# Up-projection of the latents in a two-block transformer kernel: each token tile scaled right behind its own sums of squares, tile 0 transposed while the last tile is scaled

## The reference, cut to what matters

```python
def rms_norm(x, g):
    y = xf * lax.rsqrt(jnp.mean(xf * xf, axis=-1, keepdims=True) + EPS)
    return (y * g.astype(jnp.float32)).astype(x.dtype)
def latent_attention(cq, ckv, k_rope, pos, g_cq, w_q_up, g_ckv, w_kv_up, g_qn, g_qr, g_kn, g_kr):
    ...
    q = (rms_norm(cq, g_cq) @ w_q_up).reshape(B, S, H, MLA_NOPE + MLA_ROPE)
    q_nope = rms_norm(q[..., :MLA_NOPE], g_qn)
    q_rot = rope(rms_norm(q[..., MLA_NOPE:], g_qr), pos)
    kv = (rms_norm(ckv, g_ckv) @ w_kv_up).reshape(B, S, H, MLA_NOPE + MLA_V)
    k_nope = rms_norm(kv[..., :MLA_NOPE], g_kn)
    v = kv[..., MLA_NOPE:]
    k_rot = rope(rms_norm(k_rope, g_kr), pos)
    ...
```

## Time and profile before

| | us |
|---|---|
| median of 3 runs | 3315.81 |
| lowest and highest of them | 3313.59, 3319.44 |
| the profiled execution, its own time | 3311.89 |
| its span in the trace | 3310.1 |
| `latent_up_phase`, layer 0, stretch 2097.9 to 2140.8 | 42.9 |
| `latent_up_phase`, layer 1, stretch 2791.0 to 2831.5 | 40.5 |

### The profile page before, as it was taken

The page is one execution under the profiler, slowest core; times in us unless marked ns, Lnnn a source line. Parts: engine busy times, 40 slices in busy tenths (PEclk is TensorE's granted clock), DMA queues, the critical chain, the costliest instruction groups (busy, mean ns, idle before and its releaser), DMA issues. The chain is left out here.

```text
span 3310.1 us, 50960 instructions
## 1 busy us (share of the span) xinstructions
PE 3045.4 (92%) x21910; PEld 2363.7 (71%) x21910; DVE 1610.3 (49%) x2276; ACT 1294.7 (39%) x1991; POOL 118.4 (4%) x215
## 2 busy tenths in 40 slices
PE   7996787799999898999999988899999898989999
PEld 5753666677777776677777776577888775678887
DVE  5313665455354448745454448654333467553332
ACT  3213343243233433743233344555333336544241
POOL 0200000010000000010000010100000100000000
PEclk9997778799999999999999989999999999999999
DMA  4310000154553222254543221012332320032322
GB/s 140 102 51 17 4 4 4 66 162 131 176 155 122 73 89 83 72 157 139 178 140 134 81 89 53 1 46 84 101 98 93 97 80 1 1 99 93 102 91 88
DMA packets 224241, 289.10 MB, mean 87 GB/s; under 512 B 7968, under 2 KB 163912, under 8 KB 217873
## 3 DMA queue, kind: packets, MB, share of 16 engines
q1 hardware_dynamic: 213728, 226.26, 21.8%
q0 software_dynamic: 8704, 55.39, 4.9%
q10 hardware_dynamic: 1584, 4.19, 0.3%
HBM read 281.62 MB, written 2.10 MB: 86 GB/s over the span
## 5 line engine op out<-in xcount | busy, mean ns | idle before, releaser
L226 DVE TENSOR_TENSOR weights_low_all<-weights,weights_high_all 128x2048 fp32r<-128x2048 f32 x196 | 450.0, 2296 | 584.8 <-ACT weights_high_all L220 577.2
L220 ACT CAST weights_high_all<-weights 128x2048 fp32r<-128x2048 f32 x196 | 373.6, 1906 | 575.2 <-PE ps L234 573.1
L232 PE MATMUL ps<-ffn_h_high,weights_high_all 128*128 128x512 f32 x704 | 278.4, 395 | 0.9 <-DVE weights_low_all L226 0.9
L233 PE MATMUL ps<-ffn_h_low,weights_high_all 128*128 128x512 f32 x704 | 274.9, 390 | 0.0
L234 PE MATMUL ps<-ffn_h_high,weights_low_all 128*128 128x512 f32 x704 | 274.8, 390 | 0.0
L232 PE MATMUL ps<-mlp_h_high,weights_high_all 128*128 128x512 f32 x512 | 200.8, 392 | 3.5 <-DVE weights_low_all L226 1.8
L234 PE MATMUL ps<-mlp_h_high,weights_low_all 128*128 128x512 f32 x512 | 199.4, 389 | 0.0
L233 PE MATMUL ps<-mlp_h_low,weights_high_all 128*128 128x512 f32 x512 | 199.3, 389 | 0.0
L232 PE MATMUL ps<-weights_high_all,mlp_hid_high 128*128 128x512 f32 x512 | 199.2, 389 | 0.0
L233 PE MATMUL ps<-weights_low_all,mlp_hid_high 128*128 128x512 f32 x512 | 199.2, 389 | 0.0
L234 PE MATMUL ps<-weights_high_all,mlp_hid_low 128*128 128x512 f32 x512 | 199.2, 389 | 0.0
(11 more groups left out here) (549 smaller groups left out, 6232.6 us busy)
## 6 DMA issues: line engine op xcount, KB each, us to landing
mod_w<-in_w_mod POOLq DMA_DIRECT2D x48, 1024.0 KB, 5.1
weights<-in_ffn_w_up SPq DMA_DIRECT2D x88, 512.0 KB, 5.0
weights<-in_w_mlp_in SPq DMA_DIRECT2D x32, 1024.0 KB, 5.5
weights<-in_w_mlp_out SPq DMA_DIRECT2D x32, 1024.0 KB, 4.9
weights<-in_ffn_w_down SPq DMA_DIRECT2D x24, 768.0 KB, 4.5
weights<-in_mix_w_in SPq DMA_DIRECT2D x13, 1024.0 KB, 5.2
weights<-in_na_w_qkv SPq DMA_DIRECT2D x12, 1024.0 KB, 5.1
weights<-in_w_in SPq DMA_DIRECT2D x12, 1024.0 KB, 5.4
```

The source lines that it names most:

```text
L220: nc.scalar.copy(st.high[s][:], st.raw[s][:]).then_inc(st.high_done, 1)
L226: nc.vector.tensor_tensor(st.low[s][:], st.raw[s][:], st.high[s][:], ALU.subtract).then_inc(st.split_done, 1)
L232: nc.tensor.matmul(out, lh, rh, start=start, stop=False)
L233: nc.tensor.matmul(out, lh, rl, start=False, stop=False)
```

## The change

Six things change, all inside `latent_up_phase`:

1. DVE calls `apply(t)` right behind the sums of tile t, no longer one tile later.
2. ACT takes the three square roots of a tile before the copy of its values; DVE waits for that copy (`v_done`) ahead of the key scaling.
3. ACT loads the square-root table at the phase's start, by a square root of one column into a spare tile.
4. POOL starts on a tile after its first scaling (`3 * t + 1`) and not after its third.
5. The transposes of tiles 0, 1 and 2 share banks 0 to 3, and those of tile 3 get banks 4 to 7 (`turn_bank`). So tile 0 waits for tile 2 to leave its banks, tiles 1 and 2 wait for the copy-out of the tile before, and tile 3 for its own scaling.
6. The copy-out of tile 0 moves forward: on DVE between the sums and the `apply` of tile 3, on ACT one group ahead of the roots of tile 3 and one behind.

```diff
+    def turn_bank(t, n):
+        return n + (4 if t == TT - 1 else 0)
@@ tensor
             for t in range(TT):
                 pe.wait_ge(rotated, 2 * t + 2)
+                if t in (0, TT - 1):
+                    up = 2 if t == 0 else TT - 1
+                    pe.wait_ge(scaled, 3 * (up + 1))
+                    pe.wait_ge(v_done, up + 1)
                 for n in range(4):
-                    b = (4 * t + n) % 8
-                    if t < 2:
-                        if n == 0:
-                            pe.wait_ge(scaled, 3 * (t + 3))
-                            pe.wait_ge(v_done, t + 3)
-                    else:
-                        pe.wait_ge((out_act, out_dve)[n % 2], 2 * (t - 2) + n // 2 + 1)
+                    if t in (1, 2):
+                        pe.wait_ge((out_act, out_dve)[n % 2], 2 * (t - 1) + n // 2 + 1)
@@ scalar
+            nc.scalar.activation(cx.spare[:], cx.ones[:, 0:1], ACT.Sqrt)
...
+                if t == TT - 1:
+                    put_out(0, 0)
+                roots(t)
                 nc.scalar.copy(v[:, t, :].rearrange("p (b h c) -> p b h c", b=2, h=4), heads(b + 2, P, 64, 64)).then_inc(v_done, 1)
-                roots(t)
+            put_out(0, 2)
@@ vector, in apply
+                dve.wait_ge(v_done, t + 1)
                 nc.vector.tensor_tensor(by_bank(k_tok[:, t, :, 0:64]), heads(b + 2, P, 0, 64), factor(t, 1, 64), ALU.mult)\
@@ vector, the loop
-                if t:
-                    apply(t - 1)
-            apply(TT - 1)
-            for t in range(TT):
+                if t == TT - 1:
+                    put_out(0)
+                apply(t)
+            for t in range(1, TT):
@@ gpsimd
-                pool.wait_ge(scaled, 3 * t + 3)
+                pool.wait_ge(scaled, 3 * t + 1)
```

More of the change, by code:

```diff
@@ L2927, in _ @@
                 pe.wait_ge(rotated, 2 * t + 2)
+                if t in (0, TT - 1):
+                    up = 2 if t == 0 else TT - 1
+                    pe.wait_ge(scaled, 3 * (up + 1))
+                    pe.wait_ge(v_done, up + 1)
                 for n in range(4):
-                    b = (4 * t + n) % 8
-                    if t < 2:
-                        if n == 0:
-                            pe.wait_ge(scaled, 3 * (t + 3))
-                            pe.wait_ge(v_done, t + 3)
-                    else:
-                        pe.wait_ge((out_act, out_dve)[n % 2], 2 * (t - 2) + n // 2 + 1)
+                    if t in (1, 2):
+                        pe.wait_ge((out_act, out_dve)[n % 2], 2 * (t - 1) + n // 2 + 1)
                     for h in range(4):
                         src = (q_tok, k_tok)[n // 2][:, t, 4 * (n % 2) + h, :]
-                        mm = nc.tensor.transpose(ps[0:96, b, h * P:(h + 1) * P], src, cx.ident[:])
+                        mm = nc.tensor.transpose(ps[0:96, turn_bank(t, n), h * P:(h + 1) * P], src, cx.ident[:])
                     mm.then_inc(turned, 1)
@@ L2942, in put @@
             dst = (qT, kT)[n // 2][0:96, 4 * (n % 2):4 * (n % 2) + 4, t * P:(t + 1) * P]
-            return dst, ps[0:96, (4 * t + n) % 8, :].rearrange("p (h c) -> p h c", h=4), column(cx, f"mla_{'qk'[n // 2]}{l}", 0)[0:96]
+            return dst, ps[0:96, turn_bank(t, n), :].rearrange("p (h c) -> p h c", h=4), column(cx, f"mla_{'qk'[n // 2]}{l}", 0)[0:96]
         @block.scalar
         def _(act):
+            nc.scalar.activation(cx.spare[:], cx.ones[:, 0:1], ACT.Sqrt)
             for n in (0, 2):
@@ L2956, in roots, with put_out @@
                         .then_inc(rooted, 1)
+            def put_out(t, n):
+                act.wait_ge(turned, 4 * t + n + 1)
+                dst, src, gain = put(t, n)
+                nc.scalar.activation(dst, src, ACT.Identity, scale=gain).then_inc(out_act, 1)
             for t in range(TT):
@@ L2965, in _ @@
                 nc.scalar.activation(by_bank(sq_k[t % 2]), heads(b + 2, P, 0, 64), ACT.Square).then_inc(k_sq, 1)
+                if t == TT - 1:
+                    put_out(0, 0)
+                roots(t)
                 nc.scalar.copy(v[:, t, :].rearrange("p (b h c) -> p b h c", b=2, h=4), heads(b + 2, P, 64, 64)).then_inc(v_done, 1)
-                roots(t)
-            for t in range(TT):
+            put_out(0, 2)
+            for t in range(1, TT):
                 for n in (0, 2):
-                    act.wait_ge(turned, 4 * t + n + 1)
-                    dst, src, gain = put(t, n)
-                    nc.scalar.activation(dst, src, ACT.Identity, scale=gain).then_inc(out_act, 1)
+                    put_out(t, n)
         @block.vector
@@ L2977, in _, with put_out @@
             nc.vector.tensor_scalar(cT[:, 1, :], ps[:, 1, :], column(cx, f"g_cq{l}", 1), None, ALU.mult).then_inc(lat_dve, 1)
+            def put_out(t):
+                for n in (1, 3):
+                    dve.wait_ge(turned, 4 * t + n + 1)
+                    dst, src, gain = put(t, n)
+                    nc.vector.tensor_scalar(dst, src, gain, None, ALU.mult).then_inc(out_dve, 1)
             def apply(t):
@@ L2996, in _ @@
                 nc.vector.tensor_reduce(ms[:, t, 1, :], sq_k[t % 2], AX_X, ALU.add).then_inc(sums, 1)
-                if t:
-                    apply(t - 1)
-            apply(TT - 1)
[L3000 to L3004, removed]
+                if t == TT - 1:
+                    put_out(0)
+                apply(t)
+            for t in range(1, TT):
+                put_out(t)
         @block.gpsimd
```

## The result

| | before | changed |
|---|---|---|
| median of the runs, us | 3314.7 (4 runs) | 3291.89 (4 runs) |
| lowest and highest | 3310.76, 3319.44 | 3289.78, 3294.24 |
| profiled execution, its span | 3311.89, 3310.1 | 3291.07, 3289.3 |
| phase in layer 0, in layer 1 | 42.58, 40.19 | 29.52, 29.51 |

The ratio of the times is 0.9934, with a 95% interval of 0.9922 to 0.9947. The kernel is faster by 22.8 us (0.7%), and the interval lies clear of the 0.2% that the prediction took as the bound of what can be told.

What follows compares the result with a forecast made beforehand. A chain through DVE and ACT sets the projections' pace, leaving three TensorE holes per layer. Start 2.99 plus 26.6 gives 29.6 us per layer; gains 13.0 and 10.6, together 23.6, from 3315.81 give 3292.2 us, range 3286 to 3301.

Steps and rivals of the forecast that it cites:

- the start: First latent transpose to first projection: table load 1.28, one-column root 0.23, two copies of 0.69, 0.10 to PE; 2.99 us.
- the tail: Transposes and copy-outs behind the projections, from 17.64 to the last copy-out's end at 26.6 us behind the first projection.
- the third hole: Old kernel, PE's hole ahead of the transposes in each layer, said to be a wait for the last scaling.
- No pause behind the table load: ACT at the start: roots follow the load by 0.02; rival pause of up to 1.28 per layer, 3294.8 us, chance 0.05.
- Projections without a hole: All four tiles' projections run without PE waiting, at a pace of 4.37; the last ends at 17.64 us.
- The chain of a tile: Key squares to PE's go-on: 8.64 us behind the tile's projection start, 0.10 ahead of PE's need at 8.74.
- tile 2's last group: In the tail, these transposes wait for DVE's second copy of tile 1, to 23.55, and end at 24.0 us.
- A: Clock still dips in the phase: 5.4 us of the gain lost, gain 18.2, time 3297.6 us; chance 0.20.
- B: Scaling chain misses its 0.10, tiles 2 and 3 wait again: some 1 us per layer, 3294 us; chance 0.10.
- C: ACT's copy of tile 0 delays tile 3's roots if transposes come late: half the gain lost, 3304 us; chance 0.03.
- D: TensorE's clock falls at the projections' start and stays low: 8.7 per tile for 4.37, 11 us slower, 3327; chance 0.03.
- the moved copy of the values: On ACT, now behind the roots: ends at about 7.2 us, ahead of the key scaling, so its move costs nothing.

Runs made afterwards that it cites:

- e7: Changed kernel with five alternating one-column functions, so five table loads for one, at the head of ACT's list; phase 37.68 and 37.65 us.
- e5: Changed kernel without the early one-column root, so the table load comes ahead of tile 0's roots again; phase 29.69 us in both layers.
- f2: Changed kernel with only the early scaling undone (tile t - 1 scaled behind the sums of tile t); phase 41.57 and 42.12 us, time 3311.5 us.
- g1: Changed kernel with the early one-column root moved to the end of ACT's list in the dilated attention; phase 29.13 and 29.12 us.
- f1: Kernel before with only the early scaling (each tile scaled right behind its own sums); phase 31.24 us in both layers, time 3299.2 us, ratio 0.9948.
- g4: Changed kernel measured once more, unaltered; phase 29.52 us in both layers, time 3292.3 us, ratio to the kernel before 0.9927.
- f4: Changed kernel with ACT's copy of the values ahead of the roots again; phase 29.51 us in both layers.
- e8: Changed kernel with late table load, values ahead of the roots and POOL waiting for three scalings, undone together; phase 30.82 us in both layers.

## Why the prediction was right

The forecast was 3292.2 us with a gain of 23.6; measured are 3291.89 and a gain of 22.8. The mechanism is the one forecast: the holes ahead of tiles 2 and 3 and of the transposes are gone, the half-clock time with them, and the phases are 23.74 us shorter together. That the whole time came out within 0.3 us is partly luck. The forecast started from 3315.81, 1.1 above the 3314.7 of the comparison, and its gain was 0.8 too large. Within the phase, too, two misses offset each other: the start was forecast 0.28 too long, the tail 0.2 too short.

*One reading of the old trace was off.* The prediction put the third hole down to "the last scaling". By the kernel's wait, tile 0's transposes needed tile 2's scaling, which the old order put behind the sums of tile 3; tile 3's own scaling ended after they had begun. The size of the hole and its end are the same either way.

*Start, 2.99 forecast, 2.71 measured.* ACT's two copies overlap: the row has 1.25 for both, where I added 1.38. The one-column root holds up the copies by 0.11, from 2099.51 to 2099.62, where I added 0.23, and ACT starts 0.04 ahead of PE. The copies no longer wait for a transpose each, which was their order before.

*No pause behind the table load.* 0.02 in the changed kernel, 0.01 in e7. The Trainium skill (page "ScalarE: Activation LUTs", section "What ACT_TABLE_LOAD costs") has a drain of some 1.38 us with each switch. As an estimate by that figure, the start of each layer would have been 1.38 longer. At these places the trace does not agree, and the sum by the row was the right one.

*Projections without a hole, 17.64 forecast, 17.38 measured.* Of the 0.26, 0.20 is the last tile: I took the 4.53 until its last matmul ends, and the transposes start 4.33 behind its first. The rest is tile 2, which starts 0.07 earlier than two paces of 4.37. The chain of a tile came out as added: tile 0's scaling ends at 2109.56, 8.60 behind the first projection, for 8.64; PE takes the banks at 8.67, not 8.74. With 0.05 for the handover, the slack is 0.02, so thin that the delay of tile 0's roots by 0.55 in e5 shows as 0.54 on PE. It shows once, not for every tile: each tile's chain starts from its own projection, and the interval from tile 2 to 3 in e5 is 4.40.

*Tail, 26.6 forecast, 26.81 measured* from the first projection. Its events came near the forecast times: tile 3 was to be turned from 24.0 and was from 24.11, POOL was to be done by 23.6 and was at 23.42. The waits of PE were not those forecast. I had tile 2's last group wait for DVE's second copy of tile 1. In the trace its second group waits for the first of these copies (0.55), the last group doesn't wait, and tile 1 waits for ACT by 0.47. By my own times the first of these copies would have ended at about 22.85, and three more groups behind it give 24.2, not 24.0.

*Rivals.* A did not come: the clock is 1.00 in the phase in every kernel without large holes. B did not: PE's matmuls wait for no scaling. C did not: tile 1's transposes wait for ACT by 0.47, not by more than 2. D's mechanism exists, but not where I put it: at the 1.21 us hole of this change there is no loss, at 4.22 and 7.22 there is, and then it ends with the first tile. It costs 1.7 and 2.2 us per layer there, never the 17 that I priced for the whole stretch.

*What the sum did not tell.* It priced the six edits as one. The runs share it out. The early scaling alone brings 20.3 of 23.7 us; it includes all the half-clock time of the old phases. That time can be estimated by comparing the two layers of the old trace: from tile 2 to tile 3 it took 10.65 for 7.84, from tile 3 to the transposes 9.57 for 7.88, from there to the end 9.62 for 8.36, 5.8 us together. Rival A had priced it at 5.4. It leaves 14.5 of the 20.3 for the holes themselves. The other five edits bring 1.72 per layer on top of the early scaling. Undone one at a time, the transposes and copy-outs cost 1.08, POOL's earlier start 0.66, the early load 0.18, the exchange on ACT nothing by itself and 0.5 against a late table load; these don't add up to 1.72, since each was measured with the others in place. Without the early scaling (f2) the five bring nothing. I had written that the moved copy of the values costs nothing; it also earns nothing.

*Where the phases and the whole differ.* The two phases are 23.74 us shorter between the two traces, but the spans differ by 20.8. Ahead of the first phase the changed kernel took 0.31 longer, between the phases 2.60, behind them 0.03. No instruction changed there. Between the phases, before and changed:

```profile
2140.52:2791.03 650.51, 619.05 (x3217) 490.17 (x3217) 303.45 (x427) 282.21 (x462) 10.63 (x28) 0.97 0.24 76
2127.77:2780.88 653.11, 621.49 (x3217) 492.19 (x3217) 303.31 (x427) 281.98 (x463) 10.63 (x28) 0.97 0.24 76
```

PE is busy 2.44 us longer for the same 3217 matmuls, so nearly all of the 2.60 is slower matmuls and not a new wait. In the other kernels this stretch took from 650.41 (g1) to 654.51 (f1), also with no matmul changed in it. In g4, the same program as the changed kernel, it took 652.88, so two executions of one program don't show the scatter here. The stretch ahead of the first phase varies more: the changed kernel took 2098.25 us in one profile and 2105.28 in g4. A part of that lies where the clock does: busy times from 400 to 800 us, in the changed kernel and in g4:

```profile
400.00:800.00 400.00, 330.42 (x6959) 269.17 (x6960) 219.54 (x340) 149.01 (x221) 12.26 (x25) 0.87 0.23 69
```

```profile
400.00:800.00 400.00, 330.02 (x6925) 268.18 (x6926) 216.18 (x340) 146.88 (x218) 12.26 (x25) 0.85 0.22 67
```

In the same 400 us the second has done 34 matmuls less, at a clock of 0.85 for 0.87. So I take the 2.9 us as this scatter. That is an argument from these pairs; no run isolates it. The second comparison of the same program, g4's, gives a gain of 24.2 us (3316.45 less 3292.28), and its interval, like the first one's, holds the 23.7 of the phases.

## What to carry to other kernels

Where a matrix engine waits for its banks, add up the chain that frees one tile and compare it with the pace of two tiles: here 12.1 us against 8.7, and 2.4 of the chain (f1 has 9.7) was only a neighbour's sums, and the wait for them, standing in front of it. Reorder that first; here it brought 85% of the gain, also by ending the half-clock stretches behind the holes. A small exchange on an engine that stands idle between two waits was worth nothing by itself (f4) and 0.5 us once a table load filled that idle time (e8). The table load cost nothing where its engine waited for a barrier anyway (g1).

## What the runs showed of the hardware that I had not expected

A hole of 4.22 us ahead of the projections put the next tile's 12 matmuls at a mean of 0.72 of the upper clock (6.06 us for 4.37), one of 7.22 us at 0.67, one of 1.21 us at 1.00. Of two holes of 3.27 us, 7.84 us apart, only the second was followed by half-clock matmuls in both layers of f2, and in layer 1 of the kernel before; in layer 0 of the kernel before it was the first. And two copies from PSUM on ACT that follow one another directly take 1.25 us together, not twice 0.69, an overlap of 0.13 where the prediction had left out 0.09.
